# Two blocks of a transformer on one core: head pairs prepared ahead of the attention work, and two feed-forward units fed with the residual before its norm is known

## The reference

```python
def step(S, inp):                                # the recurrence, head by head
    r_t, w_t, k_t, v_t, kk_t, a_t = inp
    sa = jnp.einsum('bhij,bhj->bhi', S, -kk_t)
    S = (S * w_t[:, :, None, :]
         + sa[..., None] * (kk_t * a_t)[:, :, None, :]
         + v_t[..., None] * k_t[:, :, None, :])
    return S, jnp.einsum('bhij,bhj->bhi', S, r_t)
...
def _conv_ffn(x, norm_ffn_g, w_up, conv_ffn_w, w_down):
    h = _rmsnorm(x, norm_ffn_g)                  # x * rsqrt(mean(x*x)) * g, token by token
    u = _causal_dwconv(h @ w_up, conv_ffn_w)     # 3 taps over the tokens
    gt, up = jnp.split(u, 2, axis=-1)
    return (jax.nn.silu(gt) * up) @ w_down
```

## Time and profile before

| | |
|---|---|
| median of 3 runs | 1468.22 us (1466.90 to 1473.95) |
| the profiled execution | 1469.24 us, span 1467.4 us |
| TensorE busy | 1408.8 us, 96% of the span |
| VectorE busy | 933.8 us, 64% |
| ScalarE busy | 487.7 us, 33% |
| GpSimd busy | 487.6 us, 33% |
| TensorE busy from 180 to 345 us | 136.5 of 165 us |
| TensorE busy from 1080 to 1115 us | 30.1 of 35 us |

### The profile page before, as it was taken

One profiled execution on the slowest core, in us unless ns is written; L12 is line 12 of the kernel. 1 busy time (PEld: TensorE's weight loads), 2 busy tenths in 40 slices (PEclk: granted clock), 3 DMA queues, 4 the chain that ended last, 5 costly groups with the idle time before them and its releaser, 6 DMA issues.

```text
span 1467.4 us, 18610 instructions
## 1 busy us (share of the span) xinstructions
PE 1408.8 (96%) x7612; PEld 1144.1 (78%) x7612; DVE 933.8 (64%) x1322; ACT 487.7 (33%) x663; POOL 487.6 (33%) x131
## 2 busy tenths in 40 slices
PE   7999978699998999999999999999989999999997
PEld 6778646587888877888888887878878888888886
DVE  6679868735413357769969974762457888885122
ACT  5443367243324232122222223322233333332121
POOL 0004110012535323343434433334423443443441
PEclk9999999799999999999999999999989999999999
DMA  6221000023314211232232231222222223222221
GB/s 206 87 87 58 29 2 2 4 85 118 129 71 144 87 58 58 86 100 102 86 105 97 87 115 58 86 98 104 86 87 86 87 88 113 87 99 95 84 96 58
DMA packets 21349, 125.14 MB, mean 85 GB/s; under 512 B 2384, under 2 KB 3408, under 8 KB 7696
## 3 DMA queue, kind: packets, MB, share of 16 engines
q1 hardware_dynamic: 20752, 121.71, 23.6%
q10 hardware_dynamic: 512, 2.23, 0.4%
HBM read 121.84 MB, written 2.10 MB: 84 GB/s over the span
## 4 chain that ended last, share of the span: by engine, by line
PE 88%; DVE 8%; ACT 3%; issue 1%; DMA 0%; DVEq 0%; SPq 0%; ACTq 0%
PE bank L402 25%; PE bank L404 24%; PE bank L403 24%; PE bank L1008 1%; PE bank L1024 1%; PE bank L354 1%; DVE conv_b L2406 1%; PE bank L393 1%; ACT prob L1409 1%; PE bank L877 1%; PE bank L958 1%; PE bank L626 0%; ACT probT L1415 0%; PE bank L362 0%; DVE op_hi L1736 0%
## 5 line engine op out<-in xcount | busy, mean ns | idle before, releaser
L1204 POOL TENSOR_TENSOR w_lo<-w_raw,w_hi 128x2048 fp32r<-128x2048 f32 (+1 forms) x102 | 468.2, 4590 | 762.8 <-ACT w_hi L1256 746.9
L402 PE MATMUL bank<-op_hi,w_hi 128*128 128x512 f32 x1344 | 529.8, 394 | 6.4 <-DVE op_lo L1758 2.3
L404 PE MATMUL bank<-op_hi,w_lo 128*128 128x512 f32 x1344 | 525.9, 391 | 0.0
L403 PE MATMUL bank<-op_lo,w_hi 128*128 128x512 f32 x1344 | 525.9, 391 | 0.0
L402 PEld LDWEIGHTS bank<-op_hi,w_hi 128*128 128x128 f32 x1344 | 253.6, 189 | 63.7 <-issue 6.3
L404 PEld LDWEIGHTS bank<-op_hi,w_lo 128*128 128x128 f32 x1344 | 253.3, 188 | 54.6
L403 PEld LDWEIGHTS bank<-op_lo,w_hi 128*128 128x128 f32 x1344 | 253.4, 189 | 54.0 <-issue 0.7
L1256 ACT ACTIVATE w_hi<-w_raw 128x2048 fp32r<-128x2048 f32 (+2 forms) x109 | 205.6, 1887 | 265.3 <-PE bank L404 265.3
L2299 DVE SCALAR_TENSOR_TENSOR bank<-pad_b,par,bank 128x512 f32<-128x512 f32 x232 | 175.3, 756 | 7.8
L2465 DVE TENSOR_TENSOR tmp<-tmp,conv_f 128x512 f32<-128x512 f32 x22 | 101.6, 4617 | 16.4 <-ACT tmp L1682 16.4
L2196 DVE TENSOR_TENSOR x_res<-bank,x_res 128x512 f32<-128x512 f32 x24 | 16.5, 691 | 136.9 <-PE bank L404 136.8
(11 more groups left out here) (374 smaller groups left out, 1702.0 us busy)
## 6 DMA issues: line engine op xcount, KB each, us to landing
w_raw<-in_w_units SPq DMA_DIRECT2D x104, 1024.0 KB, 4.9
w_raw<-in_w_units SPq DMA_DIRECT2D x4, 768.0 KB, 4.2
x_res<-in_x SPq DMA_DIRECT2D x8, 256.0 KB, 6.5
x_res<-in_x ACTq DMA_DIRECT2D x2, 1024.0 KB, 6.3
out<-x_res SPq DMA_DIRECT2D x8, 256.0 KB, 2.2
w_raw<-in_w_units SPq DMA_DIRECT2D x3, 512.0 KB, 9.0
w_raw<-in_w_units SPq DMA_DIRECT2D x4, 256.0 KB, 5.6
mem_tok<-in_mem SPq DMA_DIRECT2D x1, 1024.0 KB, 5.2
```

The lines of the kernel that those rows point to most:

```text
L402: nc.tensor.matmul(b[:, 0:width], h, xh[:, x0 + k, 0:width], start=start and k == ks[0], stop=False)
L403: nc.tensor.matmul(b[:, 0:width], h, xl(x0 + k, width), start=False, stop=False)
L404: mm = nc.tensor.matmul(b[:, 0:width], l, xh[:, x0 + k, 0:width], start=False, stop=stop and k == ks[-1])
L1204: nc.gpsimd.tensor_tensor(w_lo[u % 2][:, 0:nk, :], w_raw[u % 2][:, 0:nk, :], w_hi[u % 2][:, 0:nk, :].bitcast(F32), ALU.subtract).then_inc( ...
```

## The change

Two parts. In the first block the queues prepare pairs 1 to 3 in a new order (decays and `strict_upper` of a pair stand ahead of the attention of the pairs before it), with a second set of tiles (`prep_odd`, `decay_home`) for odd pairs. `blocks_in` and the substitution stand earlier in VectorE's queue, with `heads_out` and `maxima(3)` now between its steps and `heads_out(3)` behind `blocks_out`. The grams of chunks 0 and 1 are copied from PSUM by ScalarE and masked in place by GpSimd (`grams_masked`, 8 selects of 128x512) instead of being masked by VectorE.

At the join the operand of the first two `up` units is the residual times the norm's weight (`plain_hi` by ScalarE, `plain_lo` by VectorE), which needs no token factor. The sums for the factor are made inside the first of these units, at chunk 3, and the spread at chunk 7. The factor is copied to `rs`, and VectorE multiplies the four tiles by it in PSUM (`up_scaled`) before the taps. VectorE does this after it has formed the normed operand of the units from 2 on. Left out below are only the places where `decay_home(i, j)` stands for `prep[j]` without anything else changing.

```diff
@@ -121,6 +121,7 @@
 FIRST_POOL_UNIT = 9
+PLAIN_UNITS = 2
 MIX_ORDER = [*range(NI, CH), *range(NI)]
...
@@ -176,6 +177,7 @@
 prep = [at(f"prep{j}", R0 + 59392 + 2080 * j, [4 * 129 + 4]) for j in range(4)]
+prep_odd = [at(f"prep_odd{j}", 102400 + 2048 * j, [T]) for j in range(2)]
 qd = at("qd", R0 + 69632, [2, T])
...
@@ -243,6 +245,8 @@
 sq_f = at("sq_f", R0, [CH, T])
+plain_hi = at("plain_hi", R0 + 16384, [CH, T], F32R)
+plain_lo = at("plain_lo", 65536, [CH, T], F32R)
 pad_a = at("pad_a", R0 + 73728, [KA - 1 + T])
...
@@ -282,6 +286,9 @@
 ps = [ctx.enter_context(nc.psum_tensor(f"bank{b}", [P, T], F32)) for b in range(BANKS)]
+
+def decay_home(i, j):
+    return prep_odd[j][:, 0:T] if i % 2 else prep[j][:, 0:T]
 
...
@@ -676,8 +683,11 @@
         heads = [(NI * odd + i, P * i + HD * odd, odd, i - 2 * i2) for i in (2 * i2, 2 * i2 + 1) for odd in range(2)]
-        for odd in range(2):
-            evacuated(pe, ("gk", c, odd, i2))
+        if c < 2:
+            pe.wait_ge(sem("gram_masked"), 4 * c + 2 * i2 + 2)
+        else:
+            for odd in range(2):
+                evacuated(pe, ("gk", c, odd, i2))
         b = bank(("xv", c, i2))
...
@@ -765,21 +775,29 @@
     norms_spread(1)
+    strict_upper(0)
     scores(0)
-    strict_upper(0)
+    key_bonus(1)
+    decay_and_rate(2)
+    norms_spread(2)
     head_values()
-    key_bonus(1)
-    for p in range(1, NI):
-        head_inputs(p)
-        scores(p)
-        if p + 1 < NI:
-            decay_and_rate(p + 1)
-            norms_spread(p + 1)
-        strict_upper(p)
-        if p + 1 < NI:
-            probabilities_turned(p - 1)
-            heads_out(p - 1)
-            key_bonus(p + 1)
+    head_inputs(1)
+    key_bonus(2)
+    strict_upper(1)
+    scores(1)
+    decay_and_rate(3)
+    norms_spread(3)
+    probabilities_turned(0)
+    key_bonus(3)
+    strict_upper(2)
+    head_inputs(2)
+    strict_upper(3)
+    scores(2)
+    heads_out(0)
+    probabilities_turned(1)
+    heads_out(1)
+    head_inputs(3)
+    scores(3)
 
...
@@ -798,9 +816,9 @@
     probabilities_turned(NI - 1)
+    heads_out(NI - 1)
     token_major(1)
     value_grams(1)
-    heads_out(NI - 1)
     chunk_values(1)
...
@@ -1074,11 +1092,20 @@
         unit_tiles("wo2", i, merged_hi, plain(merged_lo), ready=None if i else "merged_ready")
-    token_sums("f", sq_f)
-    pe.wait_ge(sem("tok_f_ready"), 1)
-    spread("rs_f", tok_rs)
-    for i in range(FC):
-        unit_tiles("up", i, oh, ol, ready=None if i else "ffn_ready")
+
+    def statistics(k):
+        pe.wait_ge(sem("plain_ready"), k + 1)
+        if k == 3:
+            token_sums("f", sq_f)
+        elif k == CH - 1:
+            pe.wait_ge(sem("tok_f_ready"), 1)
+            spread("rs_f", tok_rs)
+
+    unit_tiles("up", 0, plain_hi, plain(plain_lo), ready=statistics)
+    for i in range(1, PLAIN_UNITS):
+        unit_tiles("up", i, plain_hi, plain(plain_lo))
+    for i in range(PLAIN_UNITS, FC):
+        unit_tiles("up", i, oh, ol, ready=None if i > PLAIN_UNITS else "ffn_ready")
     for i in range(4):
...
@@ -1223,6 +1250,18 @@
     nc.gpsimd.memset(invT[quarter(0), :, quarter(1)], 0.0).then_inc(sem("zeroed"), 1)
+
+    def grams_masked(c):
+        for i2 in range(2):
+            for odd in range(2):
+                h = NI * odd + 2 * i2
+                evacuated(pool, ("gk", c, odd, i2))
+                g = g_k[:, h:h + 2, :, :]
+                nc.gpsimd.affine_select(out=g, in_=g, compare_op=ALU.is_ge, fill=0.0, base=-1,
+                                        pattern=[[0, 2], [1, 2], [1, P]], channel_multiplier=-1).then_inc(sem("gram_masked"), 1)
+
+    grams_masked(0)
+    grams_masked(1)
     filled(pool, ("o", NI - 1))
...
@@ -1368,16 +1407,23 @@
     def decay_and_rate(i):
+        if i >= 2:
+            act.wait_ge(sem("prep_ready"), i - 1)
+            act.wait_ge(sem("bk_decayed"), 2 * i - 2)
+        elif i == 1:
+            filled(act, ("ga", 1, 1))
+        evac(A(decay_home(i, 0), take(act, ("z", i))[:, :], ACT.Tanh, scale=0.5, bias=half_wa[:, i:i + 1]), ("z", i))
+        evac(A(decay_home(i, 1), take(act, ("a", i))[:, :], ACT.Tanh, scale=0.5, bias=half_wa[:, NI + i:NI + i + 1]), ("a", i))
+        evacuated(act, ("a", i))
+        if i:
+            act.wait_ge(sem("rk_ready"), i)
+        A(rs[:, :], decay_home(i, 1), ACT.Identity, scale=half_ka[:, i:i + 1], bias=omka[:, i:i + 1]).then_inc(sem("rate_ready"), 1)
+
+    def decays(i):
+        act.wait_ge(sem("cum_ready"), i + 1)
         if i:
...
             act.wait_ge(sem("bk_decayed"), 2 * i)
-        evac(A(prep[0][:, 0:T], take(act, ("z", i))[:, :], ACT.Tanh, scale=0.5, bias=half_wa[:, i:i + 1]), ("z", i))
-        evac(A(prep[1][:, 0:T], take(act, ("a", i))[:, :], ACT.Tanh, scale=0.5, bias=half_wa[:, NI + i:NI + i + 1]), ("a", i))
-        evacuated(act, ("a", i))
-        A(rs[:, :], prep[1][:, 0:T], ACT.Identity, scale=half_ka[:, i:i + 1], bias=omka[:, i:i + 1]).then_inc(sem("rate_ready"), 1)
-
-    def decays(i):
-        act.wait_ge(sem("cum_ready"), i + 1)
         A(tmp[0][:, 0:516], prep[2][:, 0:516], ACT.Exp, scale=-0.5 * KAPPA).then_inc(sem("exps"), 1)
...
@@ -1424,19 +1470,33 @@
     decay_and_rate(1)
+    decays(1)
     strict_upper(0)
-    decays(1)
+    decay_and_rate(2)
+    exps(0)
+    decays(2)
     head_values()
-    exps(0)
-    for p in range(1, NI):
-        head_inputs(p)
-        if p + 1 < NI:
-            decay_and_rate(p + 1)
-        strict_upper(p)
-        if p + 1 < NI:
-            turned(p - 1)
-            decays(p + 1)
-            exps(p)
+    head_inputs(1)
+    strict_upper(1)
+    decay_and_rate(3)
+    exps(1)
+    decays(3)
+    turned(0)
+    strict_upper(2)
+    head_inputs(2)
+    strict_upper(3)
+    turned(1)
+    exps(2)
+    head_inputs(3)
+
+    def value_grams(c):
+        for i2 in range(2):
+            if c:
+                filled(act, ("yv", c - 1, i2))
+            for odd in range(2):
+                h = NI * odd + 2 * i2
+                b = take(act, ("gk", c, odd, i2))[:, :].rearrange("p (n a t) -> p n a t", n=2, a=2)
+                evac(A(g_k[:, h:h + 2, :, :], b, ACT.Copy), ("gk", c, odd, i2))
 
...
@@ -1472,9 +1532,11 @@
 
+    value_grams(0)
     chunk_values(0)
...
     token_major(1)
+    value_grams(1)
     chunk_values(1)
...
@@ -1667,6 +1729,7 @@
             evacuated(act, ("wo2", i, c % 2))
+            A(plain_hi[:, c, :], x_res[:, c, :], ACT.Copy, scale=pcol("norm_ffn_g_2", c)).then_inc(sem("plain_hi"), 1)
             A(sq_f[:, c, :], x_res[:, c, :], ACT.Square).then_inc(sem("sq_f"), 1)
...
@@ -1674,6 +1737,8 @@
                 act.wait_ge(sem("act_ready"), i - 1)
+            if i < PLAIN_UNITS:
+                act.wait_ge(sem("up_scaled"), 2 * i + m + 1)
 
...
@@ -1961,20 +2026,24 @@
         b = take(dve, ("kkr", i))
-        evac(V.scalar_tensor_tensor(prep[0][:, 0:T], kt[:, i, :], pcol("k_k", i), b[:, :], ALU.mult, ALU.mult), ("kkr", i))
+        evac(V.scalar_tensor_tensor(decay_home(i, 0), kt[:, i, :], pcol("k_k", i), b[:, :], ALU.mult, ALU.mult), ("kkr", i))
         evacuated(dve, ("kkr", i))
...
             .then_inc(sem("rk_ready"), 1)
-        V.scalar_tensor_tensor(prep[1][:, 0:T], prep[1][:, 0:T], 1.0, prep[0][:, 0:T], ALU.add, ALU.mult).then_inc(sem("b_ready"), 1)
+        V.scalar_tensor_tensor(decay_home(i, 1), decay_home(i, 1), 1.0, decay_home(i, 0), ALU.add, ALU.mult).then_inc(sem("b_ready"), 1)
+
+    def bonus_value(i):
+        b = take(dve, ("bonus", i))
+        evac(V.tensor_tensor(bonus_v[:, i, :], b[:, :], vf[:, i, :], ALU.mult), ("bonus", i))
 
...
                         ALU.mult)
-        V.scalar_tensor_tensor(chunked(ar[:, i, 0, :]), chunked(prep[0][:, 0:T]), -2.0, e_down[:, :, 0:P], ALU.mult, ALU.mult)
-        b = take(dve, ("bonus", i))
-        evac(V.tensor_tensor(bonus_v[:, i, :], b[:, :], vf[:, i, :], ALU.mult), ("bonus", i))
+        V.scalar_tensor_tensor(chunked(ar[:, i, 0, :]), chunked(decay_home(i, 0)), -2.0, e_down[:, :, 0:P], ALU.mult, ALU.mult)
+        if i != 2:
+            bonus_value(i)
         dve.wait_ge(sem("rk_ready"), i + 1)
...
@@ -2078,28 +2147,28 @@
     decayed(1)
-    for p in range(1, NI - 1):
-        if p >= 2:
-            heads_out(p - 2)
-        maxima(p)
-        probs(p - 1)
-        key_terms(p + 1)
-        decayed(p + 1)
-    heads_out(NI - 3)
-    maxima(NI - 1)
-    probs(NI - 2)
+    key_terms(2)
+    bonus_value(2)
+    maxima(1)
+    decayed(2)
+    probs(0)
+    key_terms(3)
+    decayed(3)
+    maxima(2)
+    probs(1)
     blocks_in()
-    substitution(0, 8)
-    probs(NI - 1)
-    value_grams(0, 0)
-    value_grams(0, 1)
+    substitution(0, 9)
+    heads_out(0)
+    heads_out(1)
+    maxima(3)
+    probs(2)
+    substitution(9, 16)
     heads_out(NI - 2)
-    substitution(8, 16)
-    value_grams(1, 0)
-    value_grams(1, 1)
+    probs(3)
+    substitution(16, 24)
+    substitution(24, BLK - 1)
+    blocks_out()
     heads_out(NI - 1)
-    substitution(16, BLK - 1)
-    blocks_out()
```

(11 more changed lines are left out.)

4 lines of the change are left out of this document (2 added, 2 removed).

## The result

Seven runs of the changed kernel have a median of 1486.06 us (1476.48 to 1488.33); seven runs of the kernel before beside them 1469.98 us (1466.90 to 1473.95). The ratio is 1.009, with a 95% interval of 1.007 to 1.011: 13 us slower, where 3 were forecast, and outside the range. The medians lie further apart, 16 us, because three of the seven runs took 1476.5 to 1481.1 us, at a mean granted clock of 0.977, and four took 1486.1 to 1488.3 us, at 0.972 or 0.973. The profiled execution took 1481.1 us, its span 1479.4 against 1467.4.

What follows compares the result with a forecast made beforehand. The prediction took TensorE, with gaps in its queue, to bound the kernel. It summed -2 for the first block and +5 for the join to +3, 1472.2 us profiled and 1471.3 for the median, range 1461 to 1477.

Steps and rivals of the forecast that it cites:

- What bounds the kernel before: TensorE carries the kernel; gaps of 12.6 us before the first block's side products and 10.4 us between `wo2` and `up`.
- Part A: First block, pairs first and masks on GpSimd: `blocks_in` almost 20 us earlier, but only 2 us gained overall.
- The walk: First block's four queues stepped from 176 with eight PSUM banks in turn; 1.9 us added at the end as latency.
- The first stall: Inside `probabilities_turned(1)`: TensorE stands from 222.7 to 229.6 until `heads_out(0)` frees a bank; 1.8 us added for half clock.
- Selects and lock: GpSimd's eight mask selects, 0.75 us each, six falling in VectorE's substitution and holding it up by 1.8 us.
- The second stall: Inside `value_grams(1)`: TensorE stands from about 263 to 270.0 for a bank behind `blocks_out`; 1.8 us for half clock.
- The clock recovering: At the first block's side products: five microseconds of work ahead restore full clock; up to 3.8 us gained, half taken.
- Part B: Join: `up` 0 ends 8.5 us earlier, but an 11 us gap before `up` 2 makes a loss of 4.8, call it 5.
- (1): First block: banks do not stop TensorE, the pairs-first half is worth about 12 us, total 1461; chance 0.12.
- (2): Join: `w_lo` of `up` 2 is ready in time, so the 8.5 us gain stays, total 1458; chance 0.07.
- (3): Long, blocking selects: first block loses 3 us, join loses 6, total 1477; chance 0.14.
- (4): First block and join: the change only moves waits, both halves near nothing, total 1468; chance 0.12.

Runs made afterwards that it cites:

- the join kernels: Five kernels, each the kernel before with only the join half of the change, in various queue orders; medians from 1463.85 to 1477.39 us.
- the kernel with the bank freed: Kernel before plus the first-block half of the change, with `heads_out(0)` moved ahead of the first nine substitution steps; 1463.34 us, ratio 0.9939.
- the kernel with the masks back: First-block half against the kernel before, `heads_out(0)` and `heads_out(3)` moved earlier, masks of chunks 0 and 1 on VectorE again; 1461.36 us, ratio 0.9933.
- the mended kernels: Kernels with the first-block half or the whole change, `heads_out` read-outs moved earlier, against the kernel before; medians from 1455.15 to 1466.79 us.
- the first block alone: The kernel before with only the first-block half of the change; 1479.74 us against 1471.81, ratio 1.0055.
- the join with four reorderings: Join half against the kernel before: early weights, earlier `up` 0 read-outs, later weights moved up, norm's sums split in three; 1463.85 us, ratio 0.9926.

## Why the prediction was wrong, step by step

**What bounds the kernel before** held: both gaps closed.

**Part A, up to `blocks_in`.** Forecast at 220.1 (the terms that it names add up to 219.8). At 171 the trace of after runs 2.7 us ahead of that of before (the last projection product at 171.27 against 173.93, and at 170.9 to 172.2 in the join kernels, whose first block is that of before, so this is scatter), so its 221.86 is 224.5 in the times of the forecast, 4.4 late. The walk knew only VectorE's own instructions and two waits, 2.2 and 4.6. The trace has 2.73 and 6.36, two waits for `bonus` of 1.13 and 0.41, and just ahead of the 6.36 a halved clock from 208.4 to 211.9 that the walk had not at all (row 208.31: two instructions 1.97, at full clock 1.02). A pause of 2.29 and one of 2.01 in TensorE had come before it. The 1.9 us that the walk adds as latency are the difference of two sums; no row shows their cause.

**The first stall.** Mechanism and length right: TensorE stood 6.91 us where 6.9 were forecast, released by `heads_out(0)`. What follows was undersized: transposes, products and masses at half clock cost 3.4 more (1.94, 4.54 and 1.38 against 1.07, 2.37 and 1.07 in the kernel with the bank freed), where I had added 1.8. I took the 1.8 from the earlier trace rows, where the clock was back after nine products, 3.9 us; here it stayed down through the work until 239.2.

**Selects and lock.** A select of 128x512 takes 0.69 us (four in 2.78), where 0.75 was taken. Three instructions of the substitution beside them lasted 0.68, 0.74 and 0.74 in place of 0.42, some 0.9 us in all, where 1.8 was in the sum; only four of the eight selects met the substitution, not six. The Trainium skill (SBUF — State Buffer, section "SBUF: two separate sides") has a VectorE instruction with two SBUF inputs and a GpSimd instruction that reads SBUF exclude each other; the trace agrees for a select, as it did for a subtraction, but with 0.69 us for each the price is small. What the walk left out lay elsewhere: two more handovers on TensorE's path. I had costed the moved masks as work taken off VectorE and never asked how long TensorE waits for a gram (2.07 us ahead of 256.85); the kernel with the masks back shows that the 4.9 us were no gain.

**The second stall.** Right in its cause, not in its size. Forecast from 263 to 270.0; it lasted 3.97 us, since TensorE too came late, and ended at 273.68, 276.3 in the forecast's times. The grams and value products behind it took 4.1 us more than at full clock (9.3 against 5.3 in the kernel with the first bank freed, durations added up), not 1.8.

**The clock recovering.** This step fell outright. I let the clock come back before the side products, a gain of 2 us. It stayed at 1.2 GHz from 273.3 to 290.4, through products of 64 to 256 columns and 32x32 blocks with no idle time once they had begun: 17.1 us, as long as behind the gap of before. It is the mended kernels that get this gain: with the first bank freed the side products take 2.21 us in place of 3.62. The bounds, -7 to +3, did not hold the first block's 8.1 (5.3 to 10.9), because both ends took the clock for a short tail behind each stall. Part of the 8.1 may be scatter: the profiled execution of the first block alone has half clock for 13.7 us from 297.8, that of after for 3.4.

**Part B.** Right in mechanism, each link, and in the gap (10.99). The missing 1.8 us are the half clock from 1092 to 1096 behind `token_sums`, in a unit without idle time; taking the block of one-column matmuls apart gave back 1.6 in the traces. The step that failed is "24 products to 1092.9", costed at full clock.

**The sum.** -2 and +4.8 should have been +8.1 and +5.7. In the trace of after part A is 7.0 us behind before from 171 to the end of the block, 9 us from the forecast. Terms of the clock make 7.6 of these 9: 1.7 at 208, 1.6 behind the first stall, 2.3 behind the second, and the 2.0 of a recovery that never came. They lie in one direction because they are one omission: I took the clock's fall for a fixed 1.8 us behind each long gap, while the stretches at half clock in the first block of after last 3.4, 10.2, 17.1 and 3.4 us, the first and the last of them behind pauses of some 2 us only. What sets their length stays open.

**The rivals.** (1), banks that do not bind, was refuted for this change and is what the kernel became once one read-out was moved, worth 9 us where 12 were named. (2) failed for the reason given against it. The 8.5 us that it names are real: the join with four reorderings gets exactly them (67.31 less 58.81). (3) gave the right sign by a wrong cause; selects are short. (4), both parts near nothing, is outside the interval.

## What to carry to other kernels

When a long chain is moved ahead in an engine's queue, look for every bank or buffer release that now stands behind it, and move these short read-outs in front: here 1.4 us of read-out decided over 15 us. Work started early on one engine pays only when each queue that feeds its successor is reordered too; the wait stood at three places in turn (weights, banks, weights), and only with the third repair was the join faster than before. Cost small matmuls and pauses on TensorE with each product's duration at both levels of the clock, as a range, since the same instructions had the clock at half for 3.4 or 13.7 us; and do not count work taken off an engine that is waiting there.
